# Gated norm in a hybrid diffusion block: sums with tokens on partitions, and six of eight mixed chunks split during the attention

## The reference

```python
def gated_rmsnorm(y, z, w):
    g = (y * silu(z)).reshape(Bsz, L, SSD_GROUPS, -1)
    g = g * lax.rsqrt(jnp.mean(g * g, axis=-1, keepdims=True) + EPS)
    return g.reshape(Bsz, L, SSD_INNER) * w
...
mix_x = jnp.concatenate([pool_x, ssd_x, attn_x], axis=-1) @ w_out
xs = xs + g1x * mix_x
```

## Time and profile before

| | |
|---|---|
| time, median of 3 runs | 1668.36 us (1665.81 to 1670.21) |
| profiled execution, span | 1668.2 us |
| TensorE busy | 1572.4 us, 94% |
| VectorE busy | 894.0 us, 54% |
| ScalarE busy | 595.9 us, 36% |
| GpSimd busy | 162.6 us, 10% |
| mean granted clock of TensorE | 0.980 |

### The profile page before, as it was taken

The page is one execution under the profiler, slowest core; times in us unless marked ns, Lnnn a source line. Parts: engine busy times, 40 slices in busy tenths (PEclk is TensorE's granted clock), DMA queues, the critical chain, the costliest instruction groups (busy, mean ns, idle before and its releaser), DMA issues.

```text
span 1668.2 us, 22489 instructions
## 1 busy us (share of the span) xinstructions
PE 1572.4 (94%) x9150; PEld 1416.7 (85%) x9150; DVE 894.0 (54%) x1191; ACT 595.9 (36%) x896; POOL 162.6 (10%) x159
## 2 busy tenths in 40 slices
PE   5899978889899999999999998997889899999999
PEld 4799857689899999999999997995778688888887
DVE  1667876655674555555544367447575533333333
ACT  4633445543622112222122236254554522232222
POOL 0140135002000000000000033014202000000000
PEclk9899989999999999999999998998999999999999
DMA  8546300002353333333332122220003233333322
GB/s 324 153 157 191 91 1 1 1 26 64 102 152 126 126 126 121 114 122 123 126 126 70 48 75 81 64 77 0 1 24 92 76 89 100 94 95 97 93 78 86
DMA packets 203581, 154.76 MB, mean 93 GB/s; under 512 B 8612, under 2 KB 189676, under 8 KB 203372
## 3 DMA queue, kind: packets, MB, share of 16 engines
q1 hardware_dynamic: 202060, 148.85, 28.8%
q10 hardware_dynamic: 1440, 4.78, 0.8%
HBM read 151.52 MB, written 2.10 MB: 92 GB/s over the span
## 4 chain that ended last, share of the span: by engine, by line
PE 84%; DVE 9%; ACT 4%; issue 2%; POOL 0%; DMA 0%; SPq 0%; DVEq 0%; ACTq 0%
PE banks L1720 68%; PE banks L1839 6%; PE banks L1989 1%; PE banks L1956 1%; DVE neg_max L1527 1%; PE banks L1933 1%; PE banks L1865 1%; DVE mod_sum L1199 1%; DVE nrm L1271 1%; DVE h_lo L1265 1%; DVE w_lo L1174 1%; PE banks L1647 1%; PE banks L1970 1%; PE banks L1697 1%; PE banks L1660 1%
## 5 line engine op out<-in xcount | busy, mean ns | idle before, releaser
L1720 PE MATMUL banks<-h_hi,w_hi 128*128 128x384 f32 (+3 forms) x1296 | 389.1, 358 | 26.4 <-DVE h_lo L1265 16.5
L1174 DVE TENSOR_TENSOR w_lo<-raw,w_hi 128x1056 fp32r<-128x1056 f32 x184 | 246.1, 1338 | 312.3 <-ACT w_hi L805 311.6
L1720 PE MATMUL banks<-h_lo,w_hi 128*128 128x384 f32 (+3 forms) x1296 | 385.6, 356 | 0.0
L1720 PE MATMUL banks<-h_hi,w_lo 128*128 128x384 f32 (+3 forms) x1296 | 384.9, 355 | 0.0
L805 ACT ACTIVATE w_hi<-raw 128x1056 fp32r<-128x1056 f32 x184 | 198.3, 1078 | 246.6 <-PE banks L1720 220.2
L1720 PEld LDWEIGHTS banks<-h_hi,w_hi 128*128 128x128 f32 x1296 | 237.9, 190 | 55.7 <-issue 28.4
L1720 PEld LDWEIGHTS banks<-h_hi,w_lo 128*128 128x128 f32 x1296 | 240.0, 190 | 17.1
L1720 PEld LDWEIGHTS banks<-h_lo,w_hi 128*128 128x128 f32 x1296 | 239.6, 190 | 16.1
L1720 PE MATMUL banks<-g_hi,w_hi 128*128 128x384 f32 (+1 forms) x528 | 160.0, 357 | 0.0
L1720 PE MATMUL banks<-g_hi,w_lo 128*128 128x384 f32 (+1 forms) x528 | 159.1, 355 | 0.0
L1199 DVE SCALAR_TENSOR_TENSOR mod_sum<-mod_ring,cond,mod_sum 128x1024 f32<-128x1024 f32 x126 | 158.1, 1296 | 1.4
(11 more groups left out here) (207 smaller groups left out, 1973.9 us busy)
## 6 DMA issues: line engine op xcount, KB each, us to landing
raw<-in_w_dram SPq DMA_DIRECT2D x120, 512.0 KB, 3.9
mod_ring<-in_w_mod_dram SPq DMA_DIRECT2D x96, 512.0 KB, 4.9
raw<-in_w_in_dram SPq DMA_DIRECT2D x32, 512.0 KB, 4.8
raw<-in_w_out_dram SPq DMA_DIRECT2D x16, 512.0 KB, 4.2
raw<-in_w_dram SPq DMA_DIRECT2D x16, 384.0 KB, 3.3
x_in<-in_x_dram ACTq DMA_DIRECT2D x4, 512.0 KB, 8.1
out_dram<-x_out SPq DMA_DIRECT2D x8, 256.0 KB, 2.3
inv_n<-in_count_dram ACTq DMA_DIRECT2D x4, 400.0 KB, 3.1
```

The source lines that it names most:

```text
L1174: dve.tensor_tensor(w_lo[n % 2][:, :], raw[n % 4][:, :], as_f32(w_hi[n % 2][:, :]), ALU.subtract).then_inc(lo_ready, 1)
L1720: ins = pe.matmul(to(p, a, b), ws[:, w], xs(k, a, b), start=(first and q == 0), stop=(last and q == 2))
```

## The change

The matrix of ones is turned round: `gn_sq` becomes the stationary operand, 128 tokens at a time, and one column of ones the moving one. Each matmul then gives one column of sums with tokens on the partitions, and 12 columns in PSUM (8 in layer 1) hold all sums of both feature tiles. The root and the reciprocal (a new event share of `gr` on VectorE, with the semaphore `ginv_ready`) work on 128x12. To bring the result back to features on partitions, TensorE multiplies a column of `gn_r`, broadcast to 128x128, by the identity: in rounds (`gate_rounds`) of four blocks of 128 tokens, into the same PSUM bank. VectorE multiplies `mix` by that bank, in one piece where the round lies in one feature tile and in two where it doesn't. ScalarE's copies of the sums are gone.

The events of the norm are fewer: in layer 0 `gz` and `gs` in steps 9 and 10, `gr` and round 0 in step 11, rounds 1 and 2 in steps 12 and 13. In layer 1 `gz` and `gs` in steps 7 and 8, `gr` and round 0 in step 9, round 1 in step 10.

The other part is the new event `mh`: `m_hi` and `m_lo` of chunks 0 to 5 are made inside the list, one to a step, in layer 0 in steps 14 to 19 and in layer 1 in steps 11 to 16. Chunks 6 and 7 follow after the list. The wait for all attention outputs becomes one for the head that the chunk holds.

```diff
@@ -79,7 +79,7 @@
     pm_pe=2, pm_out=2, s_ready=UNITS, max_ready=UNITS, exp_ready=UNITS, p_ready=UNITS, pv_pe=UNITS,
     pv_out=2 * ATT_HEADS, g_pe=TT, cb_pe=2 * TT, gm_ready=2 * TT, d_ready=TT, d_back_ready=TT, ecum_ready=2 * TT,
     e_ready=2 * TT, w_ready=TT, w_back_ready=TT, cdec_ready=2 * TT, xdt_ready=2 * TT, y_pe=TT, y_out=2 * TT, gz_ready=2,
-    gsq_ready=2, gss_pe=4, gss_out=4, groot_ready=1, gn_done=6, m_hi_ready=KC, m_lo_ready=KC,
+    gsq_ready=2, gss_pe=2, groot_ready=1, ginv_ready=1, m_early=6, m_hi_ready=KC, m_lo_ready=KC,
 )
@@ -250,7 +250,7 @@
         x_dt = put("x_dt", [P, DIRS, 256], at=S0 + 19456)
         x_w = put("x_w", [P, 2, 256], at=S0 + 21504)
         gn_sq = put("gn_sq", [P, T], at=S0 + 9216)
-        gn_r = put("gn_r", [P, 2, T], at=S0 + 12288)
+        gn_r = put("gn_r", [P, 2, TT], at=S0 + 12288)
         h_prev = put("h_prev", [P, DIRS, TT, 256], at=M0)
         banks = stack.enter_context(nc.psum_tensor("banks", [P, 8, 512], F32))
...
@@ -476,11 +477,11 @@
                 if l < DEPTH - 1:
                     units.append((h, -1))
                 units += [(h, t) for t in range(SEQ // P)]
-            n_sp = len(spans(l))
             gates = []
             for ft in range(2):
-                gates += [("gz", ft)] + [("gs", ft, k) for k in range(n_sp)]
-            gates += [("gr",)] + [("gi", ft, a) for ft in range(2) for a in range(lat0(l), T, 256)]
+                gates += [("gz", ft), ("gs", ft)]
+            gates += [("gr",)] + [("gi", r) for r in range(len(gate_rounds(l)))]
+            early = [("mh", j) for j in range(INCS["m_early"])]
             todo = list(chunks)
             last_c, two_buffers = None, None
             for u in range(len(units) + 3):
@@ -508,11 +509,21 @@
                         ev.append(states.pop(0))
                 if gate_now and gates:
                     ev.append(gates.pop(0))
+                elif gate_now and early and (early[0][1] < 4 or u >= 3 and units[min(u, len(units) + 2) - 3][0] > early[0][1] - 4):
+                    ev.append(early.pop(0))
                 if u < len(units) and units[u][1] == 1 and units[u][0] + 1 < ATT_HEADS:
                     ev.append(("tr", "q", units[u][0] + 1))
-            ev += gates
-            assert not todo and last_c is None and not states
+            assert not todo and last_c is None and not states and not gates and not early
             return ev, units, two_buffers
+
+        def gate_rounds(l):
+
+            cols = [(ft, t) for ft in range(2) for t in range(lat0(l) // P, TT)]
+            return [cols[k:k + 4] for k in range(0, len(cols), 4)]
+
+        def gate_pieces(l):
+
+            return sum(len({ft for ft, _ in r}) for r in gate_rounds(l))
         def score_bank(u, two_buffers):
...
@@ -989,8 +1001,16 @@
                 ev, units, two_buffers = mixer_events(l)
-                nA = n_pv = n_y = n_gs = 0
+                nA = n_pv = n_y = 0
                 job_of = {}
+
+                def mixed_hi(j):
+
+                    if j == 2:
+                        act.wait_ge(gn_done, sum(gate_pieces(k) for k in range(l + 1)))
+                    if j >= 4:
+                        act.wait_ge(pv_out, l * INCS["pv_out"] + (j - 3) * n_sp)
+                    act.activation(m_hi[:, j, r0:T], mix[:, j, r0:T], ACT.Copy).then_inc(m_hi_ready, 1)
                 for e in ev:
                     if e == ("q23", 0):
                         head_root(2)
@@ -1070,21 +1090,17 @@
                     elif e[0] == "gz":
                         act.wait_ge(gz_ready, l * INCS["gz_ready"] + e[1] + 1)
                         if e[1]:
-                            act.wait_ge(gss_pe, l * INCS["gss_pe"] + len(sp_))
+                            act.wait_ge(gss_pe, l * INCS["gss_pe"] + 1)
                         act.activation(gn_sq[:, r0:T], mix[:, 2 + e[1], r0:T], ACT.Square).then_inc(gsq_ready, 1)
-                    elif e[0] == "gs":
-                        a, b = sp_[e[2]]
-                        act.wait_ge(gss_pe, l * INCS["gss_pe"] + n_gs + 1)
-                        act.activation(gn_r[:, e[1], a:b], banks[:, 6, 0:b - a], ACT.Copy).then_inc(gss_out, 1)
-                        n_gs += 1
                     elif e[0] == "gr":
-                        act.wait_ge(gss_out, l * INCS["gss_out"] + n_gs)
-                        act.activation(gn_r[:, :, r0:T], gn_r[:, :, r0:T], ACT.Sqrt, bias=eps[:, 0:1], scale=1.0 / P).then_inc(groot_ready, 1)
-
-                act.wait_ge(gn_done, l * INCS["gn_done"] + 2 * (T - r0) // 256)
-                act.wait_ge(pv_out, l * INCS["pv_out"] + n_pv)
-                for j in range(KC):
-                    act.activation(m_hi[:, j, r0:T], mix[:, j, r0:T], ACT.Copy).then_inc(m_hi_ready, 1)
+                        act.wait_ge(gss_pe, l * INCS["gss_pe"] + 2)
+                        act.activation(gn_r[:, :, r0 // P:TT], banks[:, 6, 0:2 * TT].rearrange("p (f t) -> p f t", f=2)[:, :, r0 // P:TT],
+                                       ACT.Sqrt, bias=eps[:, 0:1], scale=1.0 / P).then_inc(groot_ready, 1)
+                    elif e[0] == "mh":
+                        mixed_hi(e[1])
+
+                for j in range(INCS["m_early"], KC):
+                    mixed_hi(j)
                 for n in range(N_OUT):
@@ -1441,6 +1457,11 @@
                 nA = nB = n_st = n_y = n_pv = 0
                 scaled = -1
+                def mixed_lo(j):
+
+                    dve.wait_ge(m_hi_ready, l * INCS["m_hi_ready"] + j + 1)
+                    dve.tensor_tensor(m_lo[:, j, r0:T], mix[:, j, r0:T], as_f32(m_hi[:, j, r0:T]), ALU.subtract).then_inc(m_lo_ready, 1)
+
                 def scale_probs(u, t):
                     dve.wait_ge(exp_ready, l * INCS["exp_ready"] + u + 1)
@@ -1563,16 +1584,22 @@
                         dve.wait_ge(y_out, l * INCS["y_out"] + 2 * n_y)
                         v = mix[:, 2 + e[1], r0:T]
                         dve.tensor_tensor(v, v, silu_z[:, e[1], r0:T], ALU.mult).then_inc(gz_ready, 1)
+                    elif e[0] == "gr":
+                        dve.wait_ge(groot_ready, l * INCS["groot_ready"] + 1)
+                        dve.reciprocal(gn_r[:, :, r0 // P:TT], gn_r[:, :, r0 // P:TT]).then_inc(ginv_ready, 1)
                     elif e[0] == "gi":
-                        ft, a = e[1], e[2]
-                        dve.wait_ge(groot_ready, l * INCS["groot_ready"] + 1)
-                        link(dve.reciprocal(gn_r[:, ft, a:a + 256], gn_r[:, ft, a:a + 256]))
-                        v = mix[:, 2 + ft, a:a + 256]
-                        dve.scalar_tensor_tensor(v, v, vecs[l][:, V_SN + ft:V_SN + ft + 1], gn_r[:, ft, a:a + 256], ALU.mult, ALU.mult)\
-                            .then_inc(gn_done, 1)
-                for j in range(KC):
-                    dve.wait_ge(m_hi_ready, l * INCS["m_hi_ready"] + j + 1)
-                    dve.tensor_tensor(m_lo[:, j, r0:T], mix[:, j, r0:T], as_f32(m_hi[:, j, r0:T]), ALU.subtract).then_inc(m_lo_ready, 1)
+                        cols = gate_rounds(l)[e[1]]
+                        dve.wait_ge(gsp_pe, sum(len(gate_rounds(k)) for k in range(l)) + e[1] + 1)
+                        for ft in sorted({f for f, _ in cols}):
+                            ts = [k for k, (f, _) in enumerate(cols) if f == ft]
+                            a = P * cols[ts[0]][1]
+                            v = mix[:, 2 + ft, a:a + P * len(ts)]
+                            dve.scalar_tensor_tensor(v, v, vecs[l][:, V_SN + ft:V_SN + ft + 1],
+                                                     banks[:, 6, P * ts[0]:P * (ts[-1] + 1)], ALU.mult, ALU.mult).then_inc(gn_done, 1)
+                    elif e[0] == "mh":
+                        mixed_lo(e[1])
+                for j in range(INCS["m_early"], KC):
+                    mixed_lo(j)
                 for n in range(N_OUT):
...
@@ -1989,14 +2017,22 @@
                                 ins = pe.matmul(dst, lhs, rhs, start=(k == 0), stop=(k == len(terms) - 1))
                         ins.then_inc(y_pe, 1)
                     elif e[0] == "gs":
-                        a, b = sp_[e[2]]
                         pe.wait_ge(gsq_ready, l * INCS["gsq_ready"] + e[1] + 1)
-                        if n_gs:
-                            pe.wait_ge(gss_out, l * INCS["gss_out"] + n_gs)
+                        if e[1] == 0:
+                            pe.wait_ge(y_out, l * INCS["y_out"] + 2 * n_y)
+                        for t in range(lat0(l) // P, TT):
+                            ins = pe.matmul(banks[:, 6, TT * e[1] + t:TT * e[1] + t + 1], gn_sq[:, t * P:(t + 1) * P], ones[:, 0:1],
+                                            start=True, stop=True)
+                        ins.then_inc(gss_pe, 1)
+                    elif e[0] == "gi":
+                        if e[1]:
+                            before = sum(len({f for f, _ in r}) for r in gate_rounds(l)[:e[1]])
+                            pe.wait_ge(gn_done, sum(gate_pieces(k) for k in range(l)) + before)
```

(15 more changed lines are left out.)

## The result

The changed kernel takes 1673.95 us (median of 9 runs, 1669.17 to 1675.55); the kernel before, timed in turn with it, 1665.99 (9 runs, 1664.63 to 1670.21). The ratio is 1.0028, with its interval 1.0017 to 1.0039: 4.7 us slower (2.8 to 6.5), a loss that stays just under the 0.3% (5.0 us) set as no change, though the interval reaches past that line. The forecast was 1670.6, 3.4 us lower. Its 8-in-10 range, 1664.5 to 1675.5, holds the time; the forecast's own narrower range, 1667.5 to 1673.5, misses it by 0.45, and the number is that of rival (b), 1674.0.

What follows compares the result with a forecast made beforehand. TensorE, busy 94% of the span, was taken as the bound, so changes pay only where it waits or is slow. Layer 0 +0.6 and layer 1 +1.6 gave +2.2 on 1668.4: 1670.6 us, 8-in-10 range 1664.5 to 1675.5.

Steps and rivals of the forecast that it cites:

- rival (b): Split steps and w_out: the 1.7 us of clock stays lost and the clock falls anew, 1674.0 us; chance 0.14.
- The sums: Layer 0 steps 9 and 10: twelve one-column passes take 1.45 us, steps 5.6 and 5.8; layer 1 0.1 more a step.
- Root and first round: Layer 0 step 11: root, reciprocal, four identity matmuls and score make the step 6.35 us, where it was 5.4.
- Steps 12 and 13: Layer 0: the 8.64 us square-root step falls to 4.95, step 13 is 4.1; steps 9 to 13 total 26.8.
- the load of exp's table ... which now stands open: Layer 0 step 12 and layer 1 step 10: the load, partly covered before, adds 1.28 us before exp.
- Splits inside the attention: Layer 0 steps 14 to 18 take 22.5 us (+4.0), layer 1 steps 11 to 14 take 16.0 (+2.3).
- The circle: Split steps: neg_max, exp, m_hi, m_lo and scaling follow in a row, 4.36 us in layer 0, 3.86 in layer 1.
- The end: Last units to w_out's first product: no wait before it, 8.4 us in layer 0 (−1.4), 8.7 in layer 1 (−0.6).
- The clock: Layer 0 behind w_out's start: with the 2.7 us wait gone, the half-clock loss of 1.7 us is regained.
- (a): Split steps fit beside the units at TensorE's 3.3 to 3.4 us, making it faster, 1662.6 us; chance 0.12.
- (c): Steps 9 to 13: each TensorE-VectorE link 0.3 us longer, 2 us in layer 0, 1 in layer 1, 1673.6; chance 0.13.
- (d): Behind each table load a wait as long as the load stands open in each layer, 1673.2 us; chance 0.02.

Runs made afterwards that it cites:

- e3: Changed kernel, same instructions, with VectorE's m_lo of each chunk one step later than ScalarE's m_hi; 1658.77 us, ratio to the kernel before 0.9953.
- e4: Changed kernel plus one unused exp on ScalarE right behind the root, so exp's table loads early; 1672.01 us, ratio to the kernel before 1.0026.
- e1: Changed kernel with its new norm alone, all eight splits behind the last unit again; 1666.97 us, ratio to the kernel before 0.9998.
- e2: Kernel before with its old norm, five chunks split in the steps behind the norm's last piece; 1672.07 us, ratio to the kernel before 1.0023.
- e5: Kernel before with nothing edited, run again for a second profile; 1670.16 us.
- e8: Changed kernel with the norm's linked events a step apart, splits starting one step later, m_lo one step behind m_hi; 1650.5 us, ratio to before 0.9887.

## Why the prediction was right, point by point

**The sums.** Twelve passes took 1.50 us for 1.45 taken; at full clock steps 9 and 10 take 5.59 and 5.81 (e3), forecast 5.6 and 5.8. In the changed kernel's profile they took 5.78 and 6.43, since a half-clock stretch lies in them. That stretch was in no term of the sum.

**Root and first round.** Step 11 took 6.47 us, forecast 6.35. Root 0.27, reciprocal 0.23 and the product 0.75 came at the durations taken from shapes nearby.

**Steps 12 and 13.** 4.52 and 3.82, forecast 4.95 and 4.1. The term "the load of exp's table ... which now stands open" was there, 1.28 us before exp, but not on the path: VectorE's products and `q_T` end after exp, and with the load away (e4) the step is no shorter. The estimate was 0.7 too long over the two steps. In layer 1 the step with the open load took 4.28 for 4.4, and step 9 there 6.78 for 6.8. The total of steps 9 to 13 in layer 0, 27.02 for 26.8, is partly luck: the half-clock stretch in steps 9 to 11 made up for what steps 12 and 13 were short of.

**Splits inside the attention.** Steps 14 to 18 took 22.24 us, forecast 22.5; layer 1's steps 11 to 14 took 15.94, forecast 16.0. The circle was forecast at 4.36 and 3.86 us and took 4.35 and 3.86. That it comes from the order of the events and not from the work is shown by e3. That no loss is left without the splits is shown by e1 (0.9998), and that they make one without the new norm by e2 (+3.8). Against e1 the splits cost 7.0 us in steps 14 to 18 (22.24 against 15.22) and give 1.8 back at the end of layer 0 (8.13 against 9.91); in layer 1 they cost 2.9 (15.94 against 13.05) and give back 1.1 (8.32 against 9.44).

**The end.** 8.13 and 8.32 us, forecast 8.4 and 8.7: `w_out` starts with no wait, and 3.31 us lie between the start of the last transposes and it, where 3.56 were taken.

**The clock.** The 1.7 behind the start of `w_out` was regained in every profile, as taken. But rival (b) was partly right too: the half-clock stretch of the rebuilt steps, which I had counted away with TensorE's stop of 4.46 us, is still there, now in steps 9 to 11, in the profile shown after stops of no more than 1.12 us. And "After the 2.2 us in layer 1 `w_out` ran at 1.0" held in the first profile of before, but not in e5, where the clock stood at 0.50 from 1237.0 to 1240.2.

**The sum.** Stage 0 came to +1.9 (forecast +2.3 without the clock) and stage 1 to +0.9 (forecast +1.6). With the 1.7 behind `w_out`, 1.2 near 444 us and 0.4 ahead of the stages, the last two of which I had not looked for, and 0.1 elsewhere, the span went from 1668.2 to 1667.8, where the sum has +2.2. The timed median lies 3.4 above the forecast all the same.

The two profiles compared are not alike in their clock: before's was taken at 0.980 (its two further profiles, with spans like it, took 1669.96 and 1670.16 us, near the top of its timed runs), the changed kernel's at 0.983 (1670.04, near the bottom). At the same mean clock the times lie about 4 us apart. At 0.983 before took 1665.6 to 1666.5 us (five executions) and the changed kernel 1670.0 to 1670.5 (four); at 0.977 before took 1670.4 to 1670.6 (three) and the changed kernel 1674.0 to 1675.6 (five). Over all executions on record with their clock, before has a mean time of 1668.4 us (43) and the changed kernel 1672.2 (12). So the timed loss is there at either clock. The sum without its clock term is +3.9 (+2.3 in layer 0, +1.6 in layer 1), close to these 4 us, and not far from the 2.7 to 3.7 that the stages lost in the profiles.

The term of the sum that was mis-sized is therefore the clock's: "I take the 1.7 as regained". It was regained at the one place where I looked, but the mean clock of the executions was not raised: it is 0.980 over the 43 executions of before and 0.980 over the 12 of the changed kernel (0.977 to 0.979 in six of the nine timed here, 0.981 to 0.983 in the three later ones). Taken at nothing, the term would have made the forecast 1672.3. Why the gain behind `w_out` did not raise the mean is not shown. And that the result counts as no change is in part luck: +4.7 lies 0.3 us inside the line.

**The rivals.** (a) It asked for `m_lo` less than 2.05 us after `neg_max`; it started 2.74 after (331.06 to 333.80), as forecast (2.75). e3 is what (a) would have been, at 1.21. (b): the measured 1673.95 is its number, 1674.0, but its mechanism was only half there: a half-clock stretch stood in the rebuilt steps, none stood in the split steps of any of the four profiles, and the 1.7 behind `w_out` did not stay. (c): the links cost 0.1 more in step 11, and steps 12 and 13 were shorter than forecast; it fell. (d): after the table load ended at 311.08 the root started at 311.10, so no wait stands behind a load in the changed kernel either. The Trainium skill (ScalarE: Activation LUTs, What ACT_TABLE_LOAD costs) sets a drain of about 1.38 us there; the trace does not agree here.

## What to carry to other kernels

When work is moved into the gaps of a pipeline that several engines pass through in order, put each engine's share of it a step behind the share it needs, so that no engine waits in its own queue for a result of the same step: e3 and e8 took 9.5 and 20.1 us off the two stages of the changed kernel (11.7 and 18.5 off its span) by that alone, with not one instruction less. Count a step by its longest circle through the queues (here 4.35 us), not by the busiest engine (TensorE, 3.3). And where a kernel's executions differ by 5 us with the clock, compare many runs, and those of like mean clock with one another: the profile of before at 0.980 and that of the changed kernel at 0.983 hid a loss of about 4 us here.

## What the runs showed of the hardware

- In the profile shown, the granted clock went to 0.50 (1.2 GHz) for 3.4 us at 300.8 us in the changed kernel, after TensorE had been working since 298.67 and before that had stood for only 1.12 us. I had tied such stretches to stops of 2.7 and 4.5 us. In e8, where TensorE is without work for 0.7 and 0.04 us in the whole of the stages, both ran at 1.00 throughout.
- The time of one kernel goes with its mean granted clock from execution to execution. The changed kernel took 1669.2 to 1670.5 us at 0.983 or 0.984 (five executions), 1671.3 and 1671.9 at 0.981 and 0.979, and 1674.0 to 1675.6 at 0.977 (five); the kernel before 1664.5 to 1666.5 at 0.981 to 0.985 and 1667.4 to 1670.8 at 0.977 to 0.980.
- The same stop did not give the same clock each time: behind the wait of 2.2 us before `w_out` in layer 1 the granted clock stayed at 1.00 in two profiles of the kernel before and stood at 0.50 from 1237.0 to 1240.2 in a third (e5).
- A matmul of one column in fp32 took 0.125 us a pass (12 in 1.50), about as much as one of 24 columns (0.97 for 8 passes): fewer columns saved nothing.
- A load of exp's table put directly behind the root (312.58, 1.28 us) held up nothing in its step: VectorE's reciprocal of the root started at 312.60, beside the load, and the next activation ran 0.02 after it (313.88).
